# A further expert body for at most 32 token columns, with TensorE in four column groups

## The chip, the cores and the metric

The kernel runs on one core of one Trainium2 chip. The metric is device time in microseconds: the time of one execution of the whole program. The kernel before takes 2081.35 us, the median of three runs (2077.87 to 2083.09).

## The reference, cut to what matters

The program is a two-layer trunk in float32 on a sequence of 256 tokens with 1024 features. Layer 0 is differential attention and a dense SwiGLU; layer 1 is an mLSTM and then top-2-of-8 SwiGLU experts. Only the experts are touched by the change:

```
probs = softmax(t @ w_router + b_router)            # t: 256 x 1024
top_p, top_i = top_k(probs, 2);  top_p /= sum(top_p)
combine[token, e] = top_p where e was chosen, else 0
for e in range(8):
    y += combine[:, e:e+1] * ((silu(t @ w_gate[e]) * (t @ w_up[e])) @ w_down[e])
```

`w_gate[e]` and `w_up[e]` are 1024 x 3584, `w_down[e]` is 3584 x 1024, all float32. The 256 tokens choose 2 experts each, so there are 512 choices in all. On the inputs of the reference its router gives experts 0 to 7 these numbers of tokens: 169, 204, 5, 19, 18, 44, 8, 45.

## The kernel before, in words

Each engine has one program. The kernel gathers, for each expert, only the tokens that chose it, and computes them as a block of columns of a width that is fixed in the code. After the router VectorE writes `counts` and `order_e`: the experts in the order in which they are done. Expert 7 is always first, because its weights are requested before the routing is known; the others come as largest, smallest, second largest, second smallest and so on (`RANKS`, line 109). With the numbers above the order is: expert 7 (45 tokens), 1 (204), 2 (5), 0 (169), 6 (8), 5 (44), 4 (18), 3 (19). This text calls them place 0 to place 7.

Weights come in chunks of 2 MB (2,097,152 bytes) into a ring of 7 slots (`ring`). An expert has 21 chunks: 7 pairs of a gate chunk and an up chunk (1024 x 512 each), then 7 down chunks (512 x 1024 each). SyncE's program (lines 419 to 428) waits before each chunk until the semaphore `freed` says that the chunk which held that slot has been read, and then issues the transfer. At most 7 chunks are therefore landed or in flight and not yet read.

For an expert, TensorE (`expert` in `pe_program`, lines 1021 to 1140) does the following.
- Gather: 16 matmuls (L1034) take the chosen tokens out of `xn`. VectorE moves the result into `xg` (L1593).
- Two transposes of the scatter matrix (L1041).
- For at most 128 tokens (`tiles == 1`): seven steps. `step(j)` has, for each of 8 k-tiles, one matmul with the gate chunk (L1060) and one with the up chunk (L1061). The tokens are the stationary operand, the 512 columns of the weights move. If the width is 64, gate goes to PSUM partitions 0 to 63 and up to partitions 64 to 127 (`second_half`), so that the two matmuls use two column groups of the array. ScalarE takes the silu of the gate half (L646), VectorE multiplies it by the up half into `hx` (L1599), and `turn(j)` transposes `hx` in four 128-column pieces (L1069), which ScalarE copies into `eh` (L650). `turn(j)` comes after `step(j + 1)`. The first piece of a turn is what frees chunks: `turn(0)` frees four at once (the two of step 0 and the two of step 1), later ones two each.
- Then seven down chunks, each four k-tiles of two matmuls (L1109), in the same two column groups. The result goes through `ye`, copied half by ScalarE (L663) and half by VectorE (L1612).
- Scatter: matmuls (L1137) with the scatter matrix, which VectorE adds into `y_sum` (L1620).
- Over 128 tokens (`tiles == 2`) the weights are the stationary operand instead (L1090), and the tokens move.

A float32 `pe.matmul` call appears in the trace as two weight loads (PEld) and two matmuls (PE), a transpose as one and one.

Which body runs is chosen at run time. Every engine's program has a loop over the 8 places (L1145 on TensorE), and in it a tree of `If`/`Else` on the number of tokens (`by_width`, lines 687 to 711). TensorE has a body for each width in `WIDTHS` (64, 128, 144, ... 256), the other engines one for each in `COARSE` (64, 128, 192, 256). The part under an `If` follows the branch in the code and ends with a jump over the `Else` part. The tree's first question is whether the number is over 64; the 64 body is in the `Else` part, after all others and right before the end of the loop. Branches of the outermost question have line 706, those of the questions further in have line 699, and the jump back to the loop's head has line 1145.

Of the kernel before, what the change touches and what calls it, by code (L numbers as in the profile page):

```python
# [19 lines left out]
ALU = mybir.AluOpType  # L20
# [6 lines left out]
P = 128  # L27
D = 1024
KT = D // P
# [77 lines left out]

RANKS = [0] + [(i + 1) // 2 if i % 2 else E - i // 2 for i in range(1, E)]
STEP = WC // P
WIDTHS = [P // 2] + list(range(P, S + 1, 16))  # L110
COARSE = [P // 2, P, P + P // 2, S]


class Count:
# [10 lines left out]
def trunk(nc, a, out):  # L125
    with ExitStack() as ctx:
# [386 lines left out]
        def act_program(act):  # L513
# [121 lines left out]
            def expert(e, width):  # L635
                tiles, sw = shape_of(width)
                act.wait_ge(scat_full, e + 1)
                act.activation(scat[:, 0:tiles, :],
                               ps[:, 4, 0:tiles * S].rearrange("p (t s) -> p t s", t=tiles), ACT.Copy).then_inc(scat_ready, 1)
                if tiles == 1:  # L640
                    for j in range(EJ + 1):
                        if j < EJ:
                            act.wait_ge(step_full, step_count(e, j))
                            if j >= 2:
                                act.wait_ge(turn_full, step_count(e, j - 2))
                            act.activation(hx[0:width, j % 2, 0:WC], ps[0:width, 2 * (j % 2)], ACT.Silu).then_inc(silu_moe, STEP)  # L646
                        if j:
                            m = j - 1
                            act.wait_ge(turn_full, step_count(e, m))
                            act.activation(eh[:, STEP * m:STEP * j, 0:width],  # L650
                                           ps[:, 6 + m % 2].rearrange("p (c s) -> p c s", c=STEP)[:, :, 0:width],
                                           ACT.Copy).then_inc(turn_free, STEP)
                else:
                    for ft in range(ET):
                        act.wait_ge(step_full, ft_count(e, ft))
                        act.activation(eh[:, ft, 0:width], ps[:, ft % UB, 0:width], ACT.Silu).then_inc(silu_moe, 1)  # L656
                    act.nop().then_inc(turn_free, ET)
                act.wait_ge(freed, e * EC + (SLOTS + EC))
                for st in range(tiles):
                    for n in range(tiles):  # L660
                        r = second_half(sw[st]) if n else slice(0, sw[st])
                        src = ps[r, 4 + 2 * st + n]
                        ins = act.activation(ye[0:sw[st], st, n * 512:(n + 1) * 512], src, ACT.Copy)  # L663
                ins.then_inc(ye_ready, 1)
# [25 lines left out]
        def by_width(eng, e, body, widths):  # L690

            n = eng.value_load(counts[0:1, bass.ds(e, 1)], min_val=0, max_val=S)

            def choose(wider):
                if len(wider) == 1:
                    body(e, wider[0])
                    return
                half = len(wider) // 2
                with eng.If(n > wider[half - 1]):
                    choose(wider[half:])  # L700
                    eng.nop()
                with eng.Else():
                    choose(wider[:half])
                    eng.nop()

            with eng.If(n > widths[0]):
                choose(widths[1:])
                eng.nop()
            with eng.Else():
                body(e, widths[0])  # L710
                eng.nop()


        def pe_program(pe):
# [306 lines left out]
            def expert(e, width):  # L1021
# [25 lines left out]
                def step(j):  # L1047

                    arrived(2 * j)
                    arrived(2 * j + 1)  # L1050
                    if j >= 2:
                        pe.wait_ge(hx_ready, step_count(e, j - 2))
                    wg, wu = slot_up((2 * j) % SLOTS), slot_up((2 * j + 1) % SLOTS)
                    b = 2 * (j % 2)
                    low = second_half(width)
                    for k in range(KT):
                        if j == 0 and k >= KT // 2 and k % 2 == 0:
                            pe.wait_ge(xg_ready, e * (KT // 2) + (k // 2 + 1))
                        x_k = xg[:, k, 0:width]
                        pe.matmul(ps[0:width, b], x_k, wg[:, k, :], start=(k == 0), stop=(k == KT - 1))  # L1060
                        ins = pe.matmul(ps[low, b + 1], x_k, wu[:, k, :], start=(k == 0), stop=(k == KT - 1))  # L1061
                    ins.then_inc(step_full, STEP)

                def turn(j, chunks_read):
                    pe.wait_ge(hx_ready, step_count(e, j))
                    if j >= 2:
                        pe.wait_ge(turn_free, step_count(e, j - 2))
                    for c in range(STEP):
                        ins = pe.transpose(ps[:, 6 + j % 2, c * P:(c + 1) * P], hx[:, j % 2, c * P:(c + 1) * P], ident[:])  # L1069
                        if c == 0 and chunks_read:  # L1070

                            ins.then_inc(freed, chunks_read)
                    ins.then_inc(turn_full, STEP)
# [21 lines left out]
                def down(j):  # L1095

                    c = 2 * EJ + j
                    arrived(c)
                    if tiles == 1:
                        pe.wait_ge(turn_free, step_count(e, j))  # L1100
                    else:
                        pe.wait_ge(hx_ready, step_count(e, j))
                    w = slot_down(c % SLOTS)
                    for st in range(tiles):
                        for k in range(DK):
                            ft = DK * j + k
                            for n in range(2):
                                r = second_half(sw[st]) if n else slice(0, sw[st])
                                ins = pe.matmul(ps[r, 4 + 2 * st + n], eh[:, ft, st * P:st * P + sw[st]],  # L1109
                                                w[:, k, n * 512:(n + 1) * 512], start=(ft == 0), stop=(ft == ET - 1))  # L1110
                                if tiles == 2 and ft == st == n == 0:
                                    ins.then_inc(freed, 2)
                    ins.then_inc(freed, 1)
# [35 lines left out]
        def dve_program(dve):  # L1149
# [437 lines left out]
            def expert(e, width):  # L1587
                tiles, sw = shape_of(width)
                for i in range(KT // 2):
                    dve.wait_ge(gather_full, e * (KT // 2) + (i + 1))  # L1590
                    for j in range(2):
                        k = 2 * i + j
                        ins = dve.tensor_scalar(xg[:, k, 0:width], ps[:, i, j * S:j * S + width], mul_c[:, 3, k:k + 1],  # L1593
                                                modc[:, 1, 24 + k:25 + k], ALU.mult, ALU.add)
                    ins.then_inc(xg_ready, 1)
                if tiles == 1:
                    for j in range(EJ):
                        dve.wait_ge(silu_moe, step_count(e, j))
                        dve.tensor_tensor(hx[0:width, j % 2, 0:WC], hx[0:width, j % 2, 0:WC],  # L1599
                                          ps[second_half(width), 2 * (j % 2) + 1], ALU.mult).then_inc(hx_ready, STEP)  # L1600
                else:
                    for ft in range(ET):
                        dve.wait_ge(silu_moe, ft_count(e, ft))
                        dve.tensor_tensor(eh[:, ft, 0:width], eh[:, ft, 0:width], ps[:, ft % UB, S:S + width],  # L1604
                                          ALU.mult).then_inc(hx_ready, 1)

                dve.wait_ge(scat_full, e + 1)
                select(e + 1)
                if tiles == 1:

                    dve.wait_ge(freed, e * EC + (SLOTS + EC))
                    dve.tensor_copy(ye[0:width, 0, 512:1024], ps[second_half(width), 5]).then_inc(half_ready, 1)  # L1612
                else:
                    dve.nop().then_inc(half_ready, 1)
                dve.wait_ge(y_added, e + 1)
                dve.wait_ge(spread, e + 1)
                for t in range(TT):
                    for c in range(2):
                        r = slice(c * 512, (c + 1) * 512)
                        ins = dve.tensor_tensor(y_sum[:, t, r], y_sum[:, t, r], ps[:, 4 + 2 * t + c], ALU.add)  # L1620
                ins.then_inc(y_added, 1)
# [63 lines left out]
```

## Time and profile before

| | us |
|---|---|
| median of three runs | 2081.35 (2077.87 to 2083.09) |
| the profiled execution | 2078.44 |
| its span, first to last instruction | 2076.7 |
| TensorE matmul busy in it | 1718.5 (83%) |
| TensorE weight load busy | 1057.4 |
| VectorE busy | 476.0 |
| ScalarE busy | 187.1 |
| moved by DMA | 483.28 MB, 233 GB/s over the span |

The eight experts run from 869 us to 2064 us of the span. The chain of work that ended last has TensorE for 71% of the span, DMA for 11%, VectorE for 7% and "issue", time in which an engine waited for nothing that the profile shows, for 6%. Branches and jumps of an engine's sequencer are not counted as busy; they can be found by their line, with the engine's name followed by a q (PEldq).

### The profile page before, as it was taken

To read this page: it belongs to the slowest core of one execution; us is meant where nothing else is said; L and a number is where in the kernel's file an instruction comes from. 1 tells how busy PE (TensorE), PEld (TensorE's weight loads), DVE (VectorE), ACT (ScalarE), POOL (GpSimd) and SP (SyncE) were. 2 spreads that over 40 slices of the span, in tenths; PEclk is the share of its full clock that TensorE was granted. 3 is DMA by queue.
4 is the path that set the end of the run, shared out by engine and by line. 5 is a ranking of instruction groups with operands and counts; after the bars stand their busy time and mean duration, and the time that the engine had idled before them with its cause. 6 is when DMAs were issued, how large, how long until landed. Compare 5 with 4: busy or idle time off the path is not lost.

```text
span 2076.7 us, 18497 instructions
## 1 busy us (share of the span) xinstructions
PE 1718.5 (83%) x7558; PEld 1057.4 (51%) x7559; DVE 476.0 (23%) x1045; ACT 187.1 (9%) x404; POOL 33.0 (2%) x70
## 2 busy tenths in 40 slices
PE   0497789999877979587999997869999787877886
PEld 0384468864755744333999433249953333332331
DVE  0586326430465340401000001010000101010102
ACT  0103210000100110110100000000000001000000
POOL 0000000000011000000000000000000000000000
PEclk9998899999899989699999998989999899999998
DMA  9595129774320106189654542995565399999996
GB/s 311 166 346 220 41 71 371 267 299 146 122 82 1 41 1 246 39 327 400 236 212 162 202 146 102 398 368 204 203 252 193 130 401 388 397 392 394 396 390 246
DMA packets 219005, 483.28 MB, mean 233 GB/s; under 512 B 17546, under 2 KB 20003, under 8 KB 218915
## 3 DMA queue, kind: packets, MB, share of 16 engines
q1 hardware_dynamic: 205090, 481.46, 62.6%
q10 hardware_dynamic: 13824, 0.47, 0.5%
q8 instruction: 75, 1.23, 0.3%
q14 instruction: 16, 0.12, 0.0%
HBM read 480.86 MB, written 1.05 MB: 232 GB/s over the span
## 4 chain that ended last, share of the span: by engine, by line
PE 71%; DMA 11%; DVE 7%; issue 6%; ACTq 2%; ACT 1%; SPq 1%; POOL 1%; DVEq 0%; POOLq 0%
PE ps L792 16%; PE ps L1090 14%; PE ps L1060 13%; PE ps L1109 9%; DMA ring<-in_moe_w_down 7%; PE ps L779 7%; DMA ring<-in_moe_w_up 4%; PE ps L1034 2%; PE ps L1137 2%; PE ps L821 1%; DVE arena L1177 1%; ACTq L554 1%; SPq L400 1%; PE ps L1069 1%; DVE hT L1211 1%
## 5 line engine op out<-in xcount | busy, mean ns | idle before, releaser
L1060 PE MATMUL ps<-ring,arena 128*64 128x512 f32 x672 | 318.2, 631 | 62.7 <-issue 48.4
L1109 PE MATMUL ps<-ring,arena 128*64 128x512 f32 (+3 forms) x1120 | 323.1, 597 | 32.2 <-DMA ring<-in_moe_w_down 32.1
L792 PE MATMUL ps<-hT,ring 128*128 128x256 f32 x1472 | 329.1, 385 | 9.0 <-DVE hT L1211 7.6
L1061 PE MATMUL ps<-ring,arena 128*64 128x512 f32 x672 | 318.7, 631 | 0.0
L792 PEld LDWEIGHTS ps<-hT,ring 128*128 128x128 f32 x1472 | 282.7, 193 | 52.1 <-DVE hT L1211 8.8
L1090 PE MATMUL ps<-arena,ring 128*128 128x208 f32 (+1 forms) x1792 | 291.5, 326 | 0.0
L1090 PEld LDWEIGHTS ps<-arena,ring 128*128 128x128 f32 x1792 | 291.2, 190 | 0.0
L1109 PEld LDWEIGHTS ps<-ring,arena 128*64 128x64 f32 (+3 forms) x1120 | 110.1, 147 | 235.2 <-issue 178.9
L1060 PEld LDWEIGHTS ps<-ring,arena 128*64 128x64 f32 x672 | 94.1, 145 | 249.7 <-issue 239.3
L779 PE MATMUL ps<-ring,arena 128*128 128x512 f32 x368 | 161.1, 600 | 1.8 <-DVE arena L1344 1.8
L1177 DVE SCALAR_TENSOR_TENSOR arena<-ring,cond,arena 128x512 f32<-128x512 f32 x168 | 126.3, 752 | 6.0
L779 PEld LDWEIGHTS ps<-ring,arena 128*128 128x128 f32 x368 | 70.9, 193 | 91.8 <-issue 89.8
L1599 DVE TENSOR_TENSOR arena<-arena,ps 64x512 f32<-64x512 f32 x42 | 29.0, 690 | 375.3 <-ACT arena L646 375.3
L1061 PEld LDWEIGHTS ps<-ring,arena 128*64 128x64 f32 x672 | 94.0, 145 | 0.0
L1034 PE MATMUL ps<-arena 128*128 128x128 f32 (+2 forms) x256 | 46.6, 359 | 47.6 <-issue 41.0
L1604 DVE TENSOR_TENSOR arena<-arena,ps 128x256 f32<-128x256 f32 (+1 forms) x56 | 21.7, 388 | 270.0 <-ACT arena L656 270.0
L1034 PEld LDWEIGHTS ps<-arena 128*128 128x128 f32 x256 | 44.9, 255 | 55.7 <-issue 47.4
L736 PE MATMUL ps<-arena,ones_col 128*32 128x128 f32 x192 | 10.5, 306 | 72.3 <-DVE arena L1177 72.3
L1620 DVE TENSOR_TENSOR arena<-arena,ps 128x512 f32<-128x512 f32 x32 | 19.9, 682 | 214.7 <-PE ps L1137 214.7
L646 ACT ACTIVATE arena<-ps 64x512 f32<-64x512 f32 x42 | 24.8, 590 | 315.8 <-PE ps L1061 315.7
L1137 PE MATMUL ps<-arena 64*128 64x512 f32 (+3 forms) x80 | 44.1, 691 | 9.7 <-DVE arena L1612 5.3
L478 POOL TENSOR_TENSOR small<-small 128x1 f32<-128x1 f32 (+2 forms) x21 | 15.7, 746 | 1927.6 <-DVE small L1201 1650.5
(262 smaller groups left out, 875.6 us busy)
## 6 DMA issues: line engine op xcount, KB each, us to landing
ring<-in_moe_w_gate SPq DMA_DIRECT2D x56, 2048.0 KB, 19.5
ring<-in_moe_w_up SPq DMA_DIRECT2D x56, 2048.0 KB, 19.5
ring<-in_moe_w_down SPq DMA_DIRECT2D x56, 2048.0 KB, 21.3
ring<-in_mod_w SPq DMA_DIRECT2D x24, 2048.0 KB, 11.8
ring<-in_mlstm_w_in SPq DMA_DIRECT2D x8, 2048.0 KB, 8.2
ring<-in_attn_w_in SPq DMA_DIRECT2D x6, 2048.0 KB, 10.5
ring<-in_ffn_w_gate SPq DMA_DIRECT2D x5, 2048.0 KB, 12.9
ring<-in_ffn_w_up SPq DMA_DIRECT2D x5, 2048.0 KB, 11.9
```

What stands on the lines that cost most here:

```text
L646: act.activation(hx[0:width, j % 2, 0:WC], ps[0:width, 2 * (j % 2)], ACT.Silu).then_inc(silu_moe, STEP)
L779: ins = pe.matmul(ps[:, 4 + 2 * t + c], lhs[:, first + k, t * P:(t + 1) * P], w[:, k, c * 512:(c + 1) * 512], start=(first + k == 0), stop ...
L792: ins = pe.matmul(dst, w[:, k, c * P:(c + 1) * P], hT[:, k, :], start=(k == 0), stop=(k == KT - 1))
L1034: ins = pe.matmul(ps[:, i, j * S:j * S + wide], xn[:, t, k * P:(k + 1) * P], sel[:, t, 0:wide], start=(t == 0), stop=(t == TT - 1))
L1060: pe.matmul(ps[0:width, b], x_k, wg[:, k, :], start=(k == 0), stop=(k == KT - 1))
L1061: ins = pe.matmul(ps[low, b + 1], x_k, wu[:, k, :], start=(k == 0), stop=(k == KT - 1))
L1090: ins = pe.matmul(dst, w[:, k, c * P:(c + 1) * P], xg[:, k, 0:width], start=(k == 0), stop=(k == KT - 1))
L1109: ins = pe.matmul(ps[r, 4 + 2 * st + n], eh[:, ft, st * P:st * P + sw[st]], w[:, k, n * 512:(n + 1) * 512], start=(ft == 0), stop=(ft == E ...
L1137: ins = pe.matmul(ps[:, 4 + 2 * t + n], scat[0:sw[st], st, t * P:(t + 1) * P], ye[0:sw[st], st, n * 512:(n + 1) * 512], start=(st == 0), s ...
L1177: ins = dve.scalar_tensor_tensor(out=acc, in0=w[:, k], scalar=cond[:, k:k + 1], in1=acc, op0=ALU.mult, op1=ALU.add)
L1599: dve.tensor_tensor(hx[0:width, j % 2, 0:WC], hx[0:width, j % 2, 0:WC], ps[second_half(width), 2 * (j % 2) + 1], ALU.mult).then_inc(hx_rea ...
L1604: dve.tensor_tensor(eh[:, ft, 0:width], eh[:, ft, 0:width], ps[:, ft % UB, S:S + width], ALU.mult).then_inc(hx_ready, 1)
```

## The change

`WIDTHS` and `COARSE` get a first entry of 32 (`Q`), and `by_width` gets one more level: the first question is now whether the number is over 32, the second whether it is over 64. The 64 body is in the `Else` part of the second question, the 32 body in the `Else` part of the first, behind it. So a body of more than 64 ends with a jump over the 64 body and then one over the 32 body, and the 64 body ends with a jump over the 32 body.

In the 32 body four column groups of 32 are used. Each k-tile of a step has four matmuls over 256 columns (left and right half of gate, left and right half of up) in place of two over 512; each k-tile of down has four output groups of 256 columns in place of two of 512, all in PSUM bank 4. The silu and the product work on 64 partitions x 256 columns, a turn has two transposes in place of four, and the last copies are two each of 32 x 256 on ScalarE and VectorE.

```
-WIDTHS = [P // 2] + list(range(P, S + 1, 16))
-COARSE = [P // 2, P, P + P // 2, S]
+Q = P // 4
+WIDTHS = [Q, P // 2] + list(range(P, S + 1, 16))
+COARSE = [Q, P // 2, P, P + P // 2, S]
...
             with eng.If(n > widths[0]):
-                choose(widths[1:])
+                with eng.If(n > widths[1]):
+                    choose(widths[2:])
+                    eng.nop()
+                with eng.Else():
+                    body(e, widths[1])
+                    eng.nop()
                 eng.nop()
             with eng.Else():
                 body(e, widths[0])
...  # TensorE, step(j), for each k
+                        if width == Q:
+                            for q in range(4):
+                                w = (wg, wg, wu, wu)[q][:, k, (q % 2) * 256:(q % 2 + 1) * 256]
+                                ins = pe.matmul(ps[q * Q:(q + 1) * Q, b, 0:256], x_k, w, start=(k == 0), stop=(k == KT - 1))
+                            continue
...  # TensorE, turn(j)
-                    for c in range(STEP):
+                    for c in range(2 if width == Q else STEP):
...  # TensorE, down(j), for each k
+                            for q in range(4 if width == Q else 0):
+                                ins = pe.matmul(ps[q * Q:(q + 1) * Q, 4, 0:256], eh[:, ft, 0:Q], w[:, k, q * 256:(q + 1) * 256],
+                                                start=(ft == 0), stop=(ft == ET - 1))
-                            for n in range(2):
+                            for n in range(0 if width == Q else 2):
...  # ScalarE
+                            if width == Q:
+                                act.activation(hx[0:2 * Q, j % 2, 0:WC // 2], ps[0:2 * Q, 2 * (j % 2), 0:WC // 2],
+                                               ACT.Silu).then_inc(silu_moe, STEP)
...
+                if width == Q:
+                    for q in range(2):
+                        ins = act.activation(ye[0:Q, 0, q * 256:(q + 1) * 256], ps[q * Q:(q + 1) * Q, 4, 0:256], ACT.Copy)
+                    ins.then_inc(ye_ready, 1)
+                    return
...  # VectorE
+                        if width == Q:
+                            dve.tensor_tensor(hx[0:2 * Q, j % 2, 0:WC // 2], hx[0:2 * Q, j % 2, 0:WC // 2],
+                                              ps[2 * Q:4 * Q, 2 * (j % 2), 0:WC // 2], ALU.mult).then_inc(hx_ready, STEP)
+                            continue
...
+                if width == Q:
+                    dve.wait_ge(freed, e * EC + (SLOTS + EC))
+                    for q in range(2, 4):
+                        ins = dve.tensor_copy(ye[0:Q, 0, q * 256:(q + 1) * 256], ps[q * Q:(q + 1) * Q, 4, 0:256])
+                    ins.then_inc(half_ready, 1)
```

## Rows read from the trace of the kernel before

**Rows 1.** The page, busy time of each engine, share of the span.
```profile
PE 1718.5 (83%) x7558; PEld 1057.4 (51%) x7559; DVE 476.0 (23%) x1045; ACT 187.1 (9%) x404; POOL 33.0 (2%) x70
```

**Rows 2.** Scatter line L1137: shortest/median/longest ns, first and last start, shapes.
```profile
L1137 PEld LDWEIGHTS ps<-arena x80: 182/187/334, 971.2 to 2062.5; 64*128 64x128 f32 x48, 128*128 128x128 f32 x16, 80*128 80x128 f32 x8, 48*128 48x128 f32 x8
```

**Rows 3.** Stretches, places 3 to 5: engines' busy us, TensorE clock, DMA share, GB/s.
```profile
1381.00:1614.00 233.00, 230.12 (x1172) 171.62 (x1172) 14.92 (x41) 14.55 (x35) 0.00 (x0) 0.96 0.60 219
1621.00:1728.00 107.00, 91.99 (x406) 36.50 (x406) 9.46 (x21) 10.34 (x18) 0.00 (x0) 0.94 0.82 311
1732.00:1840.00 108.00, 91.46 (x406) 35.13 (x406) 9.46 (x21) 10.33 (x18) 0.00 (x0) 0.95 1.04 394
```

**Rows 4.** The same view: two stretches without weights arriving, and the last 412 us.
```profile
1249.60:1286.00 36.40, 22.00 (x108) 11.30 (x108) 6.03 (x14) 3.22 (x5) 0.00 (x0) 0.77 0.02 4
1605.50:1643.60 38.10, 30.57 (x115) 14.03 (x116) 6.02 (x14) 3.22 (x5) 0.00 (x0) 0.71 0.02 3
1643.00:2055.00 412.00, 337.79 (x1498) 126.24 (x1496) 40.80 (x86) 36.66 (x67) 0.00 (x0) 0.95 1.04 392
```

**Rows 5.** SyncE's queue in order of time: start, us, what was issued.
```profile
1642.62 0.37 SPq L396 DMA_DIRECT2D ring<-in_moe_w_up  x1
...
1752.76 0.37 SPq L396 DMA_DIRECT2D ring<-in_moe_w_up  x1
```

**Rows 6.** The chain of waits, at three ends of experts: start, us, what.
```profile
1250.14 14.40 issue
...
1613.92 7.53 issue
...
1720.21 3.68 PE ps L1109 x16
...
1724.76 3.67 PE ps L1137 x8
1728.43 3.99 issue
```

**Rows 7.** Groups of line, 1628.3 to 1642.3: busy us, mean ns, idle before.
```profile
L1060 PE MATMUL ps<-ring,arena 128*64 128x512 f32 x32 | 13.9, 594 | 0.0
L1061 PE MATMUL ps<-ring,arena 128*64 128x512 f32 x32 | 13.9, 594 | 0.0
```

**Rows 8.** Line L736, 134.6 to 135.1: four groups of 32 columns, columns as Rows 2.
```profile
L736 PEld LDWEIGHTS ps<-arena,ones_col x16: 106/110/110, 134.6 to 134.9; 128*32 128x32 f32 x16
L736 PE MATMUL ps<-arena,ones_col x16: 272/273/298, 134.6 to 135.0; 128*32 128x128 f32 x16
```

**Rows 9.** TensorE in order of time, the gather of place 6.
```profile
1840.06 3.84 PE L1034 MATMUL ps<-arena 128*128 128x128 f32 x32
```

**Rows 10.** TensorE's branches by line and stretch, columns as Rows 2.
```profile
L706 PEldq COMPARE_BRANCH  x1: 4672/4672/4672, 1253.9 to 1253.9; - x1
...
L706 PEldq COMPARE_BRANCH  x1: 4701/4701/4701, 1610.5 to 1610.5; - x1
...
L1145 PEldq COMPARE_BRANCH  x1: 238/238/238, 971.3 to 971.3; - x1
...
L1145 PEldq COMPARE_BRANCH  x1: 6232/6232/6232, 1367.3 to 1367.3; - x1
...
L1145 PEldq COMPARE_BRANCH  x1: 6239/6239/6239, 1724.9 to 1724.9; - x1
...
L1145 PEldq COMPARE_BRANCH  x2: 207/214/222, 1836.6 to 1948.3; - x2
...
L699 PEldq COMPARE_BRANCH  x3: 65/73/6162, 972.6 to 978.9; - x3
```

**Rows 11.** The chain of waits inside place 2, between two steps.
```profile
1300.51 3.19 issue
1303.70 1.09 PE ps L1060
```

**Rows 12.** The chain of waits, the last scatter of the program.
```profile
2059.83 3.68 PE ps L1137 x8
```

More of the change, by code:

```diff
@@ L645, in expert @@
                                 act.wait_ge(turn_full, step_count(e, j - 2))
-                            act.activation(hx[0:width, j % 2, 0:WC], ps[0:width, 2 * (j % 2)], ACT.Silu).then_inc(silu_moe, STEP)
+                            if width == Q:
+                                act.activation(hx[0:2 * Q, j % 2, 0:WC // 2], ps[0:2 * Q, 2 * (j % 2), 0:WC // 2],
+                                               ACT.Silu).then_inc(silu_moe, STEP)
+                            else:
+                                act.activation(hx[0:width, j % 2, 0:WC], ps[0:width, 2 * (j % 2)], ACT.Silu).then_inc(silu_moe, STEP)
                         if j:
@@ L649, in expert @@
                             act.wait_ge(turn_full, step_count(e, m))
-                            act.activation(eh[:, STEP * m:STEP * j, 0:width],
-                                           ps[:, 6 + m % 2].rearrange("p (c s) -> p c s", c=STEP)[:, :, 0:width],
-                                           ACT.Copy).then_inc(turn_free, STEP)
+                            if width == Q:
+                                act.activation(eh[:, STEP * m:STEP * j, 0:Q].rearrange("p (a c) s -> p c a s", a=2),
+                                               ps[:, 6 + m % 2, 0:2 * P].rearrange("p (c a s) -> p c a s", c=2, s=Q)[:, :, 0:2],
+                                               ACT.Copy).then_inc(turn_free, STEP)
+                            else:
+                                act.activation(eh[:, STEP * m:STEP * j, 0:width],
+                                               ps[:, 6 + m % 2].rearrange("p (c s) -> p c s", c=STEP)[:, :, 0:width],
+                                               ACT.Copy).then_inc(turn_free, STEP)
                 else:
@@ L1608, in expert @@
                 select(e + 1)
-                if tiles == 1:
+                if width == Q:
+                    dve.wait_ge(freed, e * EC + (SLOTS + EC))
+                    for q in range(2, 4):
+                        ins = dve.tensor_copy(ye[0:Q, 0, q * 256:(q + 1) * 256], ps[q * Q:(q + 1) * Q, 4, 0:256])
+                    ins.then_inc(half_ready, 1)
+                elif tiles == 1:
                     dve.wait_ge(freed, e * EC + (SLOTS + EC))
```

## The prediction

> **What bounds the kernel now.** I read the page first, then the experts stretch by stretch, then the chain of waits at the seams between experts. On the page TensorE looks like the bound, with 83% of the span [rows 1]. The stretches say something else. Place 3, one of the two experts with over 128 tokens, keeps TensorE busy for 230 of 233 us while weights come at 219 GB/s: TensorE sets its pace. Place 5, a narrow one, moves 394 GB/s, and from 1643 to 2055 us the mean is 392 GB/s with the DMA share at 1.04 throughout [rows 3, 4]. Nothing TensorE does inside that stretch can shorten it: a chunk of 2.097 MB takes 5.32 us at 394 GB/s, 21 of them 111.7 us, while TensorE needs under 92. So a faster narrow body pays only where weights do not come. The same view shows where that is: from 1249.6 to 1286.0 and from 1605.5 to 1643.6 the core receives 4 and 3 GB/s [rows 4]. The ring is full, and the next transfer is issued at 1642.62 [rows 5], when turn(0) of the narrow expert frees four slots. Each such hole holds, in this order: the end of a wide expert, the jumps, the gather, step 0, step 1.
>
> **Who takes the new body.** The scatter loads show six narrow experts (48 loads on 64 partitions, 8 each) and two wide ones, of 128+80 and 128+48 rows [rows 2]. The router's numbers put 5, 8, 18 and 19 tokens in places 2, 4, 6 and 7. Places 0 and 5 (45, 44) keep the 64 body. That nobody takes the new body is thereby excluded.
>
> **Part 1: steps 0 and 1 of places 2 and 4.** Both lie in a hole, so what they save is saved in full, as 14 chunks of place 2, and the 77 from place 4 to the end, follow the restart at the DMA's own pace. Two steps of 64 columns take 13.9 us: 32 records of each line, gate and up side by side, 0.434 us per record [rows 7]. In the new body a record moves 256 columns instead of 512, and four must run side by side. They do in the one place that has four groups of 32 columns: 16 matmuls over 128 columns take about 0.5 us from 134.6 on, with 273 ns each; one after the other they would take 16 x 0.27 = 4.4 us [rows 8]. So 13.9 / 2 = 6.95 us are saved per hole, 13.9 in both. The first step's silu and product follow while step 1 runs; they are smaller than before.
> The bounds: the new body hands TensorE 8 instructions (4 loads, 4 matmuls) per 0.217 us, 27 ns each. Rows 8 is a short burst that may have been queued. The densest longer stretch is a gather with 64 instructions in 3.84 us, 60 ns each [rows 9]; at that pace 8 would take 0.48 us and the steps would gain nothing. I take the full gain, because what sets the gather's pace is its columns and loads (128-column loads, in turn with the matmuls), not the hand-over. No row allows more than the half.
> The Trainium skill (TensorE: Matmul & The Clock Gate, "Wait — 56ns, not 53.3ns?") says that start-to-start of matmuls is at least about 25 ns, or 62 ns if the sequencer decodes each in software. By the first the gain stays whole; by the second four take 0.248 us, and the gain in both holes would be 12 us.
>
> **Part 2: the jump over a second body.** The way out of a wide body is a row of jumps on TensorE's sequencer. The last before the loop's end, over the 64 body, takes 4.67 us in place 1 and 4.70 in place 3 [rows 10]. They are not hidden: 14.40 and 7.53 us of idle time remain after the scatter, under "issue" [rows 6]. With the change there is one more such jump in the same chain, over a body of about 1,450 instructions. (The 64 body has about 810, counting records: 4 per matmul call, 2 per transpose.) It costs 4.7 us per hole, 9.4 in both. Place 0 has the 64 body and so far falls through to the loop's end, where the jump back takes 0.24 us [rows 10]. It now jumps over the 32 body as well, at a time when weights come at full rate; jumps from there take 6.23 and 6.24 us [rows 10]. Place 1 is bound by TensorE, so these 6.2 us are paid in full. Bounds: the short price 0.24 each (0.7 in all) and, for all three, 6.2 (18.7). I take 4.7 + 4.7 + 6.2 = 15.6. Places 1 and 3 also get one more branch not taken on entry, under 0.1 us (the short ones of L699) [rows 10].
> On this the Trainium skill (Runtime: NRT & Kernel Launch, "Instruction fetch mechanics") says that a taken branch out of the fetched window stalls until the target page has been fetched. The long rows agree; of the jumps back to the loop's head 0.21 and 6.2 us both occur, which the rule alone does not explain.
>
> **Part 3: the seam from place 4 to 5.** Today the last down chunk of place 4 has landed at 1720.2. The ring then takes 7 more chunks, until 1720.2 + 7 x 5.32 = 1757.4, and the next issue is at 1752.76 [rows 5, 6]: 4.6 us to spare, less some 2 us from issue to data. New on this path: place 5 is in the Else of the second question, a jump to a body last used at place 0, like the 6.16 us on entry to place 1 [rows 10]. The shorter down gives up to 1.8 back. A stall of 1 to 4 us follows, the bounds being 0 and 6; I take 2.5. From 5 to 6 the added jumps are made up by 6.95 us of faster steps, and from 6 to 7 nothing is added that the spare time does not cover.
>
> **Part 4: the last down chunk.** In places 2 and 7 it is on the path, 3.68 us today (as in place 4 [rows 6]); half is 1.84. But between down chunks TensorE will then be idle for 5.3 - 1.84 = 3.5 us each time, and after 3.19 us of idle time a matmul took 1.09 us instead of 0.59 [rows 11]: the clock had fallen from 2.4 to 1.2 GHz. At the low level the chunk takes as long as today, and the last scatter (3.68 us [rows 12]) could even lose 3.7. The bounds are -3.7 and +3.7. I take -1.0. The four small copies before the scatter cost 0.1 to 0.2 more than two large ones; that is in it. All other steps, turns and downs of the 32 body gain time that the weights' arrival hides; their cover is gone only if DMA became faster than TensorE.
>
> **Sum.** -13.9 + 15.6 + 2.5 - 1.0 = +3.2 us. The profiled execution took 2078.44 us (span 2076.7), so its like would take 2081.6. It lies 2.9 us under the median 2081.35; the same step from the median gives **2084.5 us**. A difference under 0.3% (6.2 us) cannot be told from no change here: the three runs before span 5.2 us.
>
> **Rivals.**
> - A, jumps are short. Jumps back to the loop's head took 0.21 us in places 5 and 6 and 0.24 in place 0 [rows 10]; if the sequencer also finds the new targets at hand, Parts 2 and 3 vanish: -13.9 - 1.0 = -14.9, **2066.5 us**. Against it: all jumps over the 64 body were long. Chance 0.20.
> - B, further misses. The loop's head is no longer at hand after place 0, because a further far jump lies between: the jump back costs 4.5 to 6.2 instead of 0.24. It falls in the same chain before place 1: about +5.4, **2089.9 us**. For it: after places 2 and 4 it did cost 6.2. Chance 0.17.
> - C, slower than before: the four groups don't go at 27 ns an instruction. From 54 ns on the steps gain nothing, and the jumps remain: +3.2 + 13.9 = +17.1, **2098.4 us**. For it: no longer stretch of the trace is denser than 60 ns [rows 9]. Against it: rows 8. Chance 0.11. It would also show if the clock stayed at the low level in steps 0 and 1, which doubles them.
>
> **How the numbers follow.** The forecast has 0.52, with its own range 2077 to 2091 from the bounds of Parts 2 to 4. The range over all, 2068 to 2095, leaves out C and the faster half of A, about 0.2. Faster by over 0.3%: A and 0.01, 0.21. Slower: C, nearly all of B and 0.07 of the forecast, 0.33. Within: 0.46.
>
> **What would show it.** Steps 0 and 1 of place 2 should take 7 us together, all records 256 columns wide, four starting within some 20 ns. Two jumps of line 706 or its new neighbour should stand at the end of places 1 and 3, each near 4.7 us, and one near 6.2 after place 0. The holes should be 2 us shorter each; the hole before place 5, absent now, should show as 1 to 4 us without issue. From the restart in place 4 to the last down chunk it should be some 2 us more than the 412 of today. Wrong would be: the holes over 6 us shorter (A), the steps still at 13.9 (C), a gap of over 14 us before place 1's gather (B; 4.3 today, 10.5 forecast).

## The result and the profile after

The changed kernel takes 2105.64 us, the median of four runs (2098.18 to 2111.12), against 2082.22 for the kernel before in its four. The ratio is 1.0113, 95% interval 1.0071 to 1.0156: some 23 us slower, where 2 to 3 us were forecast and the range ended at 2095.

The profiled execution took 2098.18 us (span 2096.4), 19.7 more than that of before. First the page of the changed kernel: busy time, the two queues that fetch instructions (packets, MB, share of 16 engines), and the first of the new lines.

```profile
PE 1615.1 (77%) x8846; PEld 1056.3 (50%) x8847; DVE 468.3 (22%) x1049; ACT 178.1 (8%) x408; POOL 33.0 (2%) x70
...
q8 instruction: 114, 1.87, 0.4%
q14 instruction: 51, 0.42, 0.1%
...
L1083 PE MATMUL ps<-ring,arena 128*32 128x256 f32 x1792 | 135.7, 471 | 84.4 <-issue 65.8
```

TensorE is busy for 103 us less than before [rows 1] and the program is slower. Line L1083 has 1792 records, which is 4 experts x 7 steps x 64: four experts took the new body. The two queues fetched 114 and 51 packets; before it was 75 and 16. That is the first sign of what went wrong.

Second, the experts part by part. The table is made from the first matmul of each gather, each first turn and the last scatter, which both timelines list. Times start at the gather of place 0, as what lies before it varies by up to 7 us from one profiled execution to the next, whichever kernel it is.

| from, to (us) | before | after | difference | forecast |
|---|---|---|---|---|
| A: gather of place 0 to gather of place 1 | 110.0 | 124.1 | +14.1 | +6.2 |
| B: on to turn(0) of place 2 | 305.5 | 302.6 | -2.9 | +4.7 - 6.95 = -2.25 |
| C: on to gather of place 3 | 96.9 | 95.3 | -1.6 | -0.5 |
| D: on to turn(0) of place 4 | 260.7 | 258.3 | -2.4 | +4.7 - 6.95 = -2.25 |
| E: on to the last scatter | 417.6 | 430.0 | +12.4 | +2.0 |

B, C and D came within 1.1 us of the forecast. A and E hold the error: 7.9 and 10.4 us.

The steps first. Steps 0 and 1 of place 2 in the changed kernel, in order of time (start, us, engine, line): 128 records in 7.11 us, where two steps took 13.9 [rows 7].

```profile
1287.42 7.11 PE L1083 MATMUL ps<-ring,arena 128*32 128x256 f32 x128
1294.47 0.44 PE L1094 MATMUL ps<-ident,arena 128*128 128x128 f32 x2
```

Part A, in the changed kernel's chain of waits, and TensorE's branches by line there (shortest/median/longest ns, start). L721 is the new jump over the 32 body, L1173 the jump back to the loop's head.

```profile
973.83 18.08 issue
991.91 3.26 PE ps L1054 x9
```

```profile
L721 PEldq COMPARE_BRANCH  x1: 6191/6191/6191, 970.2 to 970.2; - x1
...
L1173 PEldq COMPARE_BRANCH  x1: 7419/7419/7419, 976.5 to 976.5; - x1
...
L721 PEldq COMPARE_BRANCH  x1: 4667/4667/4667, 1271.1 to 1271.1; - x1
...
L721 PEldq COMPARE_BRANCH  x1: 4736/4736/4736, 1623.6 to 1623.6; - x1
...
L722 PEldq COMPARE_BRANCH  x1: 6646/6646/6646, 1737.7 to 1737.7; - x1
...
L1173 PEldq COMPARE_BRANCH  x1: 7480/7480/7480, 1853.4 to 1853.4; - x1
...
L1173 PEldq COMPARE_BRANCH  x1: 6199/6199/6199, 1962.5 to 1962.5; - x1
...
L721 PEldq COMPARE_BRANCH  x1: 6831/6831/6831, 1969.6 to 1969.6; - x1
```

The three added jumps cost 6.19, 4.67 and 4.74 us, as forecast to a tenth. But the jump back after place 0 went from 0.24 to 7.42 us [rows 10]. The gap before place 1's gather is 18.1 us, where 10.5 were forecast and over 14 was named as the sign of rival B. The same happened after places 5 and 6, where the jump back had taken 0.2 us: it now takes 7.48 and 6.20, and the entry to the body of place 7 takes 6.83 more.

Part E: stretches of the changed kernel (length, busy us of the engines, TensorE's clock, DMA share, GB/s), the whole and two short ones in it.

```profile
1649.50:2073.50 424.00, 270.23 (x2374) 128.12 (x2366) 35.22 (x87) 29.96 (x67) 0.00 (x0) 0.80 1.01 382
1761.50:1766.50 5.00, 5.00 (x26) 1.74 (x24) 0.69 (x1) 0.96 (x2) 0.00 (x0) 1.00 0.32 97
1991.50:1995.50 4.00, 4.00 (x74) 2.14 (x70) 0.85 (x2) 1.70 (x4) 0.00 (x0) 1.00 0.24 91
```

The same bytes take 424 us in place of 412 [rows 4]. Weights stop arriving twice, at the seams from place 4 to 5 and from 6 to 7. The first was forecast, though smaller (there SyncE goes 15.3 us without an issue, where it was 9.3 before), the second not. And VectorE shows something that no line of the forecast had: its sequencer, at the seam from place 5 to 6. The first three rows are at the end of its loop and behind the jump back; the last two are its jump at L721 and the first instruction behind it.

```profile
L1661 DVEq ALU_OP  x1: 40/40/40, 1851.4 to 1851.4; - x1
L1661 DVEq COMPARE_BRANCH  x1: 56/56/56, 1851.5 to 1851.5; - x1
L1661 DVEq FUSED_REGOPS  x1: 63/63/63, 1857.8 to 1857.8; - x1
...
L721 DVEq COMPARE_BRANCH  x1: 56/56/56, 1858.5 to 1858.5; - x1
...
L1618 DVEq ALU_OP  x2: 40/40/40, 1864.8 to 1864.9; - x2
```

The branches themselves read 56 ns, but 6.3 us pass after each before the next instruction starts. On VectorE a long jump stands as a hole behind the branch and not as its duration. Between the entry to place 0 and the end of place 7 there are 12 such holes of over 3 us in the changed kernel and none in the kernel before. At this seam they aren't the last thing waited for, though: TensorE's own jumps hold its gather up by 11.48 us, and its steps follow the gather at once.

```profile
1862.15 5.28 PE L1054 MATMUL ps<-arena 128*128 128x128 f32 x32 [11.48 <-issue]
1867.27 0.38 PE L1061 MATMUL ps<-ident,arena 128*128 128x128 f32 x2
```

What each engine costs can therefore not be read from this trace alone; the experiments part them.

That it is instructions that come late shows in the queues that fetch them. From 1748 us on, in place 5, to its end the changed kernel still fetches 23 and 12 packets; the kernel before fetches none from 1736 us on, in either queue.

```profile
q8 instruction: 23, 0.38, 0.5%
q14 instruction: 12, 0.10, 0.1%
```

### The profile page after: what moved, and what is told of

Same layout as the page of the kernel before. It is cut to its first block, busy times and chain, and to the rows that moved or that the text cites. A ratio compares the mean times of both kernels' runs of the same rounds, so it can differ in the third digit from the quotient of the medians.

```text
span 2096.4 us, 21105 instructions
## 1 busy us (share of the span) xinstructions
PE 1615.1 (77%) x8846; PEld 1056.3 (50%) x8847; DVE 468.3 (22%) x1049; ACT 178.1 (8%) x408; POOL 33.0 (2%) x70
## 4 chain that ended last, share of the span: by engine, by line
PE 66%; DMA 9%; issue 8%; DVE 7%; SPq 6%; ACTq 2%; ACT 1%; POOL 1%; DVEq 0%; POOLq 0%
PE ps L812 16%; PE ps L1115 14%; PE ps L1137 9%; DMA ring<-in_moe_w_down 7%; PE ps L799 7%; SPq L401 5%; PE ps L1085 5%; PE ps L1083 3%; PE ps L1054 2%; PE ps L1165 2%; DMA ring<-in_moe_w_gate 1%; PE ps L841 1%; DMA ring<-in_moe_w_up 1%; DVE arena L1205 1%; ACTq L555 1%
## 5 line engine op out<-in xcount | busy, mean ns | idle before, releaser
L1137 PE MATMUL ps<-ring,arena 128*64 128x512 f32 (+3 forms) x672 | 221.7, 596 | 11.7 <-DMA ring<-in_moe_w_down 11.7
L1083 PE MATMUL ps<-ring,arena 128*32 128x256 f32 x1792 | 135.7, 471 | 84.4 <-issue 65.8
L1137 PEld LDWEIGHTS ps<-ring,arena 128*64 128x64 f32 (+3 forms) x672 | 80.3, 154 | 148.9 <-issue 128.5
L1083 PEld LDWEIGHTS ps<-ring,arena 128*32 128x32 f32 x1792 | 71.4, 135 | 142.6 <-issue 102.1
L1085 PE MATMUL ps<-ring,arena 128*64 128x512 f32 x224 | 104.8, 625 | 15.5 <-issue 15.5
L1133 PE MATMUL ps<-ring,arena 128*32 128x256 f32 x896 | 72.6, 480 | 57.0 <-DMA ring<-in_moe_w_down 57.0
L1086 PE MATMUL ps<-ring,arena 128*64 128x512 f32 x224 | 104.9, 625 | 0.0
L1133 PEld LDWEIGHTS ps<-ring,arena 128*32 128x32 f32 x896 | 31.9, 135 | 95.2 <-DMA ring<-in_moe_w_down 69.2
L1085 PEld LDWEIGHTS ps<-ring,arena 128*64 128x64 f32 x224 | 31.2, 144 | 77.3 <-issue 76.9
L756 PE MATMUL ps<-arena,ones_col 128*32 128x128 f32 x192 | 10.5, 306 | 72.2 <-DVE arena L1205 72.2
L1628 DVE TENSOR_TENSOR arena<-arena,ps 64x256 f32<-64x256 f32 x28 | 11.8, 423 | 218.0 <-ACT arena L648 218.0
```

The costliest lines, as they stand in the source:

```text
L1083: ins = pe.matmul(ps[q * Q:(q + 1) * Q, b, 0:256], x_k, w, start=(k == 0), stop=(k == KT - 1))
L1133: ins = pe.matmul(ps[q * Q:(q + 1) * Q, 4, 0:256], eh[:, ft, 0:Q], w[:, k, q * 256:(q + 1) * 256], start=(ft == 0), stop=(ft == ET - 1))
```

## Experiments

Two theories stood at first. **S**, instruction supply: jumps whose target isn't at hand, on TensorE's longer loop. **C**, the clock: the twice as fast body leaves TensorE idle, its mean granted clock in the stretch falls from 0.95 to 0.80, and the seams come late for that. After the first four runs a third and a fourth: **V**, the same as S, but on VectorE; and **W**, the weights arrive more slowly because TensorE reads them in four groups. The letters A to E are those of the table above.

**f_split: the long body without the change.** In the kernel before, each matmul over 512 columns of the 64 body is given as two over 256.

```
-pe.matmul(ps[0:width, b], x_k, wg[:, k, :], start=(k == 0), stop=(k == KT - 1))
-ins = pe.matmul(ps[low, b + 1], x_k, wu[:, k, :], start=(k == 0), stop=(k == KT - 1))
+for r in (slice(0, 256), slice(256, 512)):
+    pe.matmul(ps[0:width, b, r], x_k, wg[:, k, r], start=(k == r.start == 0), stop=(k == KT - 1 and r.stop == 512))
+    ins = pe.matmul(ps[low, b + 1, r], x_k, wu[:, k, r], start=(k == r.start == 0), stop=(k == KT - 1 and r.stop == 512))
...  # and so in down
```

> The kernel before, with one edit: in the 64 body each matmul over 512 columns of a step or of down is given as two over 256 in the same column group. Same tree, same array time, same clock, but some 1,480 instructions in the body in place of 810. Theory S (instruction supply: the long body no longer stays at hand for the next round of the loop, so the jump back, and perhaps the entry, cost 6 to 7 us at every place): the jump back after place 0 goes from 0.24 to 6 or more, in places 5 and 6 from 0.21 to 6, and the spare time of 4.6 us at the seams after places 4, 5 and 6 is overdrawn, so that SyncE issues late; in all 8 to 18 us slower, 2090 to 2100 us. Theory C (the clock: a body that is twice as fast leaves TensorE idle, its clock falls, and gathers and restarts come late): nothing of that changes here, 2080 to 2084 us.

Measured: 2103.63 us against 2080.87, ratio 1.0098 (1.0076 to 1.0121). Length alone costs nearly what the whole change did. TensorE's branches at the seam from place 5 to 6, and the stretch:

```profile
L1151 PEldq COMPARE_BRANCH  x1: 6349/6349/6349, 1853.4 to 1853.4; - x1
...
L706 PEldq COMPARE_BRANCH  x1: 6781/6781/6781, 1860.7 to 1860.7; - x1
...
1655.40:2081.10 425.70, 340.19 (x2758) 225.74 (x2754) 40.99 (x86) 36.30 (x65) 0.00 (x0) 0.92 1.01 381
```

Before, the jump back took 0.22 us there [rows 10] and the entry 0.21. The clock is 0.92, and VectorE's code is unchanged. The loss was larger than the 2090 to 2100 us that I expected: each seam pays twice, back and in.

**e_half: the idle time without the long body.** In the kernel before, steps 2 to 6 and the downs of the 64 body leave out every second k-tile.

```
-for k in range(KT):
+ks = range(KT) if j < 2 else range(0, KT, 2)
+for k in ks:
...
+ks = range(0, DK, 2) if tiles == 1 else range(DK)
```

> The kernel before, with half of the work of the 64 body left out: steps 2 to 6 and all downs use every second k-tile (the output is therefore not the reference's); steps 0 and 1 are whole. TensorE is then as idle between chunks as in the changed kernel, with the old tree and a shorter body. Theory S: no far jump is added, so 2079 to 2084 us, and the stretch from the restart in place 4 to the last down chunk stays at 412 us. Theory C: granted clock near 0.7 in the narrow places, gathers and steps late, stalls of SyncE after places 4 and 6, the stretch 417 to 424 us and the whole 2087 to 2095 us.

Measured: 2069.08 us, ratio 0.9949 (0.9929 to 0.9968): faster than before, which neither theory had. The stretch, and TensorE's branches on the way into place 3:

```profile
1635.90:2045.90 410.00, 257.32 (x960) 90.43 (x956) 39.93 (x86) 36.27 (x65) 0.00 (x0) 0.84 1.04 394
```

```profile
L1147 PEldq COMPARE_BRANCH  x1: 226/226/226, 1370.5 to 1370.5; - x1
...
L699 PEldq COMPARE_BRANCH  x3: 70/70/213, 1371.7 to 1372.1; - x3
```

The granted clock fell to 0.84, and the weights arrive at 394 GB/s all the same, in 410 us: C is out as the cause of E. Most of the gain is at the seam into place 3: with a body of some 540 instructions the jump back takes 0.23 us and the far branch into place 3 at most 0.21, where before they took 6.23 [rows 10] and 6.60 us:

```profile
L699 PEldq COMPARE_BRANCH  x3: 70/70/6598, 1374.5 to 1381.3; - x3
```

Part C of the table falls from 96.9 to 86.0 us, and E from 417.6 to 414.6.

**c_two_steps: four groups in steps 0 and 1 only**, tree as changed.

```
-if width == Q:
+if width == Q and j < 2:
...  # the same in turn, ScalarE and VectorE; down as in the 64 body
```

> The changed kernel, with the four column groups in steps 0 and 1 only; steps 2 to 6 and down of the 32 body are as in the 64 body (two groups of 512 columns). The body has some 940 instructions in place of 1,460, and the clock stays up. Both holes keep the 7 us of faster steps. Theory S: the jumps of the tree remain (13 us after place 0, 4.7 at the end of places 1 and 3), but the shorter body stays at hand from place 6 to 7, and the stretch from the restart to the last down chunk goes from 424 to 414 to 418 us: 2092 to 2100 us. Theory C predicts the same total; if the stretch stays at 424 us with the clock up, C is out as its cause.

Measured: 2107.8 us, ratio 1.012 (1.0099 to 1.014), over the 2092 to 2100 us expected, and E at 430.4 us: no better than the change. TensorE's jump back after place 6 is as long as in the changed kernel, and only the entry to place 7 is short again:

```profile
L1173 PEldq COMPARE_BRANCH  x1: 6294/6294/6294, 1971.5 to 1971.5; - x1
...
L721 PEldq COMPARE_BRANCH  x1: 242/242/242, 1978.6 to 1978.6; - x1
```

So of the long jumps only that entry hangs on the length of the new body, and the stretch stays at 424 us without it. Neither the length nor the clock (0.90) explained E; this is where VectorE came into view.

**d_local_if: TensorE's tree as before, the choice inside the 64 body.**

```
+if width == WIDTHS[0]:
+    with pe.If(size[0] > Q):
+        step(0); step(1); pe.nop()
+    with pe.Else():
+        step(0, True); step(1, True); pe.nop()      # four groups
 for j in range(EJ):
-    step(j)
+    if width > WIDTHS[0] or j > 1:
+        step(j)
```

> The version to which the theory points: TensorE keeps the tree of the kernel before, with the 64 body, and inside that body only steps 0 and 1 stand in an If on more than 32 tokens, with an Else of the same two steps in four column groups. ScalarE and VectorE have a 32 body for it. The jump is a short one (over some 130 or 260 instructions). Theory S: both holes shrink by 7 us and nothing else moves, 2067 to 2073 us, if the short jumps cost under 1 us; if they cost 3 to 6 us each, 2076 to 2084 us. Theory C: the same 2067 to 2073 us, as the clock stays up.

Measured: 2081.97 us against 2080.87, ratio 1.0004 (0.9995 to 1.0014), not the 2067 to 2073 us expected. The local branches are short (at most 0.45 us) and B and D are 6.5 and 7.3 us shorter than before. All of it is given back in E, 430.8 us. At the seam from place 5 to 6, TensorE and then VectorE in order of time:

```profile
1830.11 3.84 PE L1060 MATMUL ps<-arena 128*128 128x128 f32 x32
1833.78 0.38 PE L1067 MATMUL ps<-ident,arena 128*128 128x128 f32 x2
1845.85 1.51 PE L1089 MATMUL ps<-ring,arena 128*32 128x256 f32 x12 [11.68 <-DVE arena L1637]
```

```profile
1830.28 2.48 DVE L1673 TENSOR_TENSOR arena<-arena,ps 128x512 f32<-128x512 f32 x4 [3.92 <-PE ps L1181]
1844.37 1.84 DVE L1637 TENSOR_SCALAR arena<-ps,mul_c,modc 128x32 f32<-128x32 f32 x8 [11.61 <-issue]
```

TensorE's gather is done at 1834.2 and its steps wait 11.68 us for `xg`, which VectorE starts 11.61 us after its last work. No data is late: VectorE has two jumps of 6.3 us to get there. Its tree still has five bodies.

**k_local_if_four_bodies: the same, with four bodies on ScalarE and VectorE.**

```
-COARSE = [Q, P // 2, P, P + P // 2, S]
+COARSE = [Q, P // 2, P, S]
```

> The local If of the run before on TensorE (tree as in the kernel before, steps 0 and 1 in four groups for at most 32 tokens), and on ScalarE and VectorE the bodies 32, 64, 128 and 256: four as in the kernel before, in place of five (the two experts with over 128 tokens take the 256 body there, 48 and 80 columns wider than needed). Theory V (VectorE's loop with five bodies no longer stays at hand; its jumps back and into the body cost 6 us each and hold up xg at the seams after places 4, 5 and 6): with four bodies no long jump on VectorE after place 0, the stretch from the restart in place 4 to the last down chunk goes back from 424 to 411 to 413 us, and the saving in the holes, 2 x 6.5 us, reaches the end: 2066 to 2071 us, ratio 0.993 to 0.995. Rival W (the stretch is 424 us because the weights themselves come slower once TensorE reads them in four groups): 2080 to 2084 us, as the run before.

Measured: 2066.52 us against 2082.09, ratio 0.9924 (0.9908 to 0.994). In place 3 ScalarE's wider body copies other rows than TensorE wrote for the right half of the second tile, so a part of one expert's output is left out; the instructions keep their number and kind. The stretch:

```profile
1633.60:2044.80 411.20, 331.15 (x1624) 127.99 (x1620) 38.36 (x85) 33.26 (x65) 0.00 (x0) 0.93 1.04 393
```

424 to 411 us by one body less: V holds, W is out, as TensorE reads the weights in four groups here too.

**h_dve_tree: the further body on VectorE alone**, all else as in the kernel before.

```
-by_width(dve, e, expert, COARSE)
+by_width(dve, e, expert, [Q] + COARSE)      # with the further level of the tree
```

> The kernel before, where VectorE's tree alone gets the further level and a further body for at most 32 tokens, which is the 64 body's code with width 32. TensorE and ScalarE are as before, nothing is in four groups. Theory V: VectorE's long jumps (0 before, 12 in the changed kernel) come back, the seams after places 4, 5 and 6 stall, the stretch goes from 412 to 422 to 425 us, the holes stay: 2090 to 2096 us. Rival W: 2080 to 2084 us.

Measured: 2094.84 us, ratio 1.0066 (1.0049 to 1.0083). A to D are those of before within 0.4 us, E is 430.8. Its instruction queues and its stretch:

```profile
q8 instruction: 75, 1.23, 0.3%
q14 instruction: 51, 0.42, 0.1%
```

```profile
1642.50:2066.90 424.40, 341.04 (x1496) 127.63 (x1492) 39.49 (x86) 36.28 (x65) 0.00 (x0) 0.92 1.01 381
```

So q14 is VectorE's, and VectorE's copy of the tree alone is enough for an E as long as that of the change.

**j_pe_tree: the further body on TensorE alone**, two groups, 64 body's code.

```
-by_width(pe, e, expert, WIDTHS)
+by_width(pe, e, expert, [Q] + WIDTHS)       # with the further level of the tree
```

> The kernel before, where TensorE's tree alone gets the further level and a further body of the 64 body's code with width 32, some 810 instructions, in two groups. This is the price of the tree on TensorE without the gain. Theory S: 13 us after place 0 (a jump over the new body, then a long jump back), 4.7 us each at the ends of places 1 and 3, 4 to 8 us in the stretch (entry to the 64 body in place 5 and the way out of it), nothing won: 2103 to 2112 us. If the jump back after place 0 stays at 0.24 us, 2097 to 2106 us.

Measured: 2118.43 us, ratio 1.0176 (1.0158 to 1.0193), 6 us over the top of what I expected. A is 124.0, as in the changed kernel: a short body doesn't save the jump back after place 0. B and D are +6.0 and +4.6. E is 428.9, with no hole of over 3 us on VectorE: TensorE's copy of the tree alone is nearly enough for it too. All its jumps back are long here, 6.2 to 7.5 us while weights arrive and some 4.6 us in the two holes.

```profile
L708 PEldq COMPARE_BRANCH  x1: 6179/6179/6179, 975.6 to 975.6; - x1
...
L1159 PEldq COMPARE_BRANCH  x1: 7463/7463/7463, 982.0 to 982.0; - x1
```

**b_one_jump: another order of the tree.**

```
-with eng.If(n > widths[0]):
-    with eng.If(n > widths[1]):
+with eng.If(n > widths[1]):
...  # wide bodies
+with eng.Else():
+    with eng.If(n > widths[0]):      # the 64 body, Else the 32 body
```

> The changed kernel with another order of the tree: the first question is whether the number is over 64, and the Else part holds a second one on 32, with the 64 body and the 32 body in it. The wide bodies then end with one jump over both, not two. Theory S: the ends of places 1 and 3 lose one jump of 4.7 us each, nothing else changes, 8 to 11 us less than the changed kernel: 2090 to 2099 us.

Measured: 2112.22 us, ratio 1.0147 (1.0125 to 1.0168): not faster than the changed kernel. The jump is saved, and the entry to the 32 body pays for it:

```profile
L725 PEldq COMPARE_BRANCH  x1: 3822/3822/3822, 1283.0 to 1283.0; - x1
...
L725 PEldq COMPARE_BRANCH  x1: 7657/7657/7657, 1984.9 to 1984.9; - x1
```

In the changed kernel the wide body's way out ends right before the 32 body, and its first instructions are then at hand (0.25 us in place 2). Here it ends before the second question, and the entry takes 3.82 us. That the place where the way out ends decides this is my reading; it was not tested by itself. E is 436.9 us.

**l_after_dve4: the changed kernel with four bodies on VectorE.**

```
-by_width(dve, e, expert, COARSE)
+by_width(dve, e, expert, [Q, P // 2, P, S])
```

> The changed kernel, with four bodies on VectorE (32, 64, 128, 256) in place of five; TensorE as in the changed kernel. Theory V and S together: VectorE's 12 long jumps vanish, TensorE's stay (18 us after place 0 in its gap, one more each at places 1 and 3, the 32 body not at hand from place 6 to 7). TensorE's misses alone were enough to stall the seams in the run with the split body, so only part of the stretch comes back: 416 to 422 us in place of 424, and 2094 to 2103 us in all, against 2105.6 of the changed kernel. If it came under 2092 us, VectorE alone would have made the stretch; if it stays at 2105 us, VectorE's misses were hidden behind TensorE's.

Measured: 2103.27 us, ratio 1.0105 (1.0091 to 1.012). The total is at the top of what was expected, and the stretch as expected:

```profile
1658.40:2078.30 419.90, 274.41 (x2374) 130.16 (x2366) 35.50 (x87) 29.99 (x67) 0.00 (x0) 0.79 1.02 386
```

E is 426.3 us. On their own VectorE's jumps cost 13 us of E; beside TensorE's they cost 4. Two late engines at one seam don't add up.

**m_local_if_dve4: all of it computed.** As d_local_if, with `[Q, P // 2, P, S]` on VectorE only.

> The version that computes all of it: TensorE with the local If (tree as in the kernel before; steps 0 and 1 in four groups for at most 32 tokens), ScalarE with five bodies (32, 64, 128, 192, 256; it had no long jump with five), VectorE with four (32, 64, 128, 256). It differs from the run with four bodies on both only in ScalarE's part of the 169-token expert. Theory V: no long jump on VectorE after place 0, holes of 30 us in place of 37, a stretch of 411 to 413 us, 2064 to 2071 us, ratio 0.991 to 0.995, faster than both kernels. If five bodies hurt on ScalarE too: 2076 us or more.

Measured: 2069.5 us against 2080.81, ratio 0.9942 (0.993 to 0.9954), faster than both kernels. Its two holes and its stretch:

```profile
1254.20:1284.30 30.10, 14.96 (x172) 10.46 (x172) 5.44 (x14) 2.70 (x5) 0.00 (x0) 0.72 0.03 5
1603.40:1634.80 31.40, 23.95 (x179) 13.41 (x180) 5.44 (x14) 2.70 (x5) 0.00 (x0) 0.65 0.03 5
1634.80:2046.10 411.30, 329.19 (x1624) 127.94 (x1620) 38.62 (x85) 33.28 (x65) 0.00 (x0) 0.93 1.04 393
```

The holes were 36.4 and 38.1 us [rows 4]. Part 1 of the prediction, 13.9 us for the four groups in two steps of two experts, is 13.7 us of spans here: 6.6 in B, 7.1 in D. ScalarE has five bodies in this run and shows no hole of over 3 us between the places.

## Why the prediction was wrong

- **What bounds the kernel: right.** From the restart in place 4 on, the transfers set the pace, and faster steps could shorten only the holes before them. TensorE's 103 us less of busy time brought next to nothing else (C: -1.6). e_half shows one more place that isn't bound by weights and that the prediction did not name: the way into place 3, 11 us.
- **Part 1, the steps: right.** 13.9 us forecast, 7.11 us for two steps measured, so 13.6 saved; the instruction pace that rival C feared (28 ns each here) was no limit.
- **Part 2, the added jumps: right in price, incomplete in number.** 4.7, 4.7 and 6.2 were forecast; 4.67, 4.74 and 6.19 came. The step that failed here is that the jump back after place 0 was left at its old price: it cost 7.42 us in place of 0.24. That is rival B, with 0.17 of the chance and a price of 5.4 where 7.2 was right. The rows for it stood ahead of the prediction (6.23 and 6.24 us after places 2 and 4, 0.24 after place 0); I counted jumps and not what the loop still has at hand. j_pe_tree shows that the jump over any further body is enough.
- **Part 3, the seams: the step that failed most.** It said that only the seam from place 4 to 5 stalls, for 2.5 us, and that "from 6 to 7 nothing is added that the spare time does not cover". E grew by 12.4 us. Two things were missing. First, TensorE's jumps back after places 5 and 6, 0.2 us before and put at nothing in the sum, cost 7.48 and 6.20, and the entry to place 7 6.83. The further body in TensorE's tree makes nearly all of E by itself (j_pe_tree, 428.9 us), and so does a long body in the old tree (f_split, 432.1 us). Second, the change adds a body to every engine's tree, and I priced jumps on TensorE alone. VectorE had no hole of over 3 us between the places, so no row of before warned; its 12 new ones make E by themselves too (h_dve_tree, 430.8 us). In the changed kernel the two lie side by side: taking VectorE's away gives only 4 of the 12 us (l_after_dve4), taking TensorE's away gives none (d_local_if, 430.8 us), and E goes back to 417.6 us only where both are gone (m_local_if_dve4). The spare time at the seam, some 2.6 to 4.6 us by my reading, is smaller than one long jump: from place 4 to 5 SyncE waits 6 us longer than before, and the DMA engines are under half busy for 3.5 us.
- **Part 4, the last chunk: forecast -1.0.** In place 2 it gained (C: -1.6), in place 7 nothing: the chunk took 3.58 us and the scatter 5.12 where it took 3.68 [rows 12], with a granted clock of 0.65 around the one and 0.71 in the other, as feared, where it was 1.00 before. From the last scatter's start to the end it is 18.3 us against 16.8.
- **The sum.** A is 7.9 us over its forecast and E 10.4; B, C and D are 1.9 us under theirs together.
- **Rivals A and C: both out.** No added jump was short, and no step was slow.

The Trainium skill (Runtime: NRT & Kernel Launch, "Instruction fetch mechanics") gives TensorE room for 2048 instructions and most other engines for 512, and says beside it that only two pages of 256 are at hand. The runs lie between. Where a round of the loop runs the same body as the round before it, one of 810 (before) or some 1,070 instructions (d_local_if) is followed by a jump back of 0.21 to 0.23 us, and one of 1,480 (f_split) by one of over 6. A look at that section for the other engines would have raised the question of VectorE.

What stays open: why the jump back after a 64 body is long after places 2 and 4 and short after 0, 5 and 6 in the kernel before. The branches of all runs show a pattern: from place 1 on, with narrow bodies of 810 instructions or more, the jump back is long whenever the place ran another body than the place before it. With 540 instructions it is short after the narrow body even then (e_half, place 2). In the changed kernel no place up to 6 runs the body of the place before it, and every jump back there is long. The cause was not settled: no run shows which part of the older instructions is given up first. Nor was the number of instructions counted at which VectorE's loop stops fitting: four bodies do, five don't.

## What to carry to other kernels

A body more in a run-time choice can be paid by every engine that has the choice (here TensorE and VectorE, and not ScalarE), and mostly outside the body: in longer ways out for the other bodies, and in loops that no longer stay at hand. Before adding one, read each engine's branches and the holes behind them, and the spare time at the seam, which one jump of 6 us can use up. A choice inside an existing body, of some 130 to 260 instructions, cost 0.2 to 0.45 us a place, and gave the gain that the new body lost.

## What the runs showed of the hardware

- A far jump on TensorE took 4.5 to 5.3 us while no weights arrived and 5.9 to 7.7 us while they did; two kinds were shorter, the entry to place 0 (3.3 to 3.8 us, no weights arriving) and the entry to the 32 body in b_one_jump (3.8 us in the holes). On VectorE, which shows it as a hole behind the branch, the jumps between the places took 2.7 to 4.1 us without weights, and with them 5.6 to 6.3 us, or 4.1 to 4.3 on the entry to place 3.
- Four groups of 32 columns run side by side at full pace: a float32 matmul of 256 columns every 0.22 us in each group, eight instructions per 0.22 us, for 7.1 us on end.
- A shorter body is worth time to its neighbours: with some 540 instructions in the narrow body, the way into the wide one lost two long jumps, 11 us (e_half).
- A granted clock of 0.84 in a stretch that waits for weights cost nothing measurable there (e_half, 410 us).
